# Two channel tiles of the next block's first product, taken ahead at the block ends of a decoder trunk

## The reference

```
h = h + c * rms_norm(block(rms_norm(h, g_pre)), g_post)
ffn:  f = (silu(a @ w_gate) * (a @ w_up)) @ w_down          # 1024 -> 2816 -> 1024, c = 1/2
mix:  proj = a @ w_in                                        # 1024 -> 2576
      mix = concat(pool(..), conv(..), gla(q, k, v, ..)) @ w_out   # c = 1
rms_norm(x, g) = x * rsqrt(mean(x * x, over channels) + 1e-6) * g
```

## Time and profile before

| | us |
|---|---|
| median of three runs | 1024.07 |
| profiled execution, its own time | 1023.6 |
| its span | 1021.8 |
| TensorE busy | 1012.9 (99%) |
| VectorE busy | 603.5 (59%) |
| ScalarE busy | 488.6 (48%) |
| GpSimd busy | 271.0 (27%) |

### The profile page before, as it was taken

The page is one execution under the profiler, slowest core; times in us unless marked ns, Lnnn a source line. Parts: engine busy times, 40 slices in busy tenths (PEclk is TensorE's granted clock), DMA queues, the critical chain, the costliest instruction groups (busy, mean ns, idle before and its releaser), DMA issues.

```text
span 1021.8 us, 21132 instructions
## 1 busy us (share of the span) xinstructions
PE 1012.9 (99%) x8870; PEld 983.0 (96%) x8870; DVE 603.5 (59%) x574; ACT 488.6 (48%) x537; POOL 271.0 (27%) x184
## 2 busy tenths in 40 slices
PE   9999999999999999999999999999999999999997
PEld 8999999989999999999999999999899999999886
DVE  5755453488966744554376454544889677455452
ACT  5543434456555544343455443434565665434331
POOL 0333330123402333330113333301234024333200
PEclk9999999999999999999999999999999999999999
DMA  9765545645345755336747553356453557565621
GB/s 295 244 213 164 161 134 186 211 126 164 126 149 164 225 186 170 128 113 198 219 130 233 180 164 128 123 191 216 126 165 127 158 157 247 175 195 202 194 77 42
DMA packets 164147, 173.85 MB, mean 170 GB/s; under 512 B 9316, under 2 KB 150888, under 8 KB 164088
## 3 DMA queue, kind: packets, MB, share of 16 engines
q1 hardware_dynamic: 161960, 171.01, 52.7%
q10 hardware_dynamic: 2128, 1.98, 0.7%
HBM read 171.91 MB, written 1.06 MB: 169 GB/s over the span
## 4 chain that ended last, share of the span: by engine, by line
PE 95%; ACT 1%; DMA 1%; DVE 1%; SPq 0%; issue 0%; DVEq 0%; ACTq 0%
PE ps L1295 24%; PE ps L1296 24%; PE ps L1297 24%; PE ps L1327 2%; PE ps L1328 2%; PE ps L1312 2%; PE ps L1416 2%; PE ps L1458 2%; PE ps L1496 2%; PE ps L1498 2%; PE ps L1497 2%; PE ps L1459 2%; PE ps L1643 1%; DMA raw<-in_ffn_wu 1%; PE ps L1525 1%; PE ps L1354 0%
## 5 line engine op out<-in xcount | busy, mean ns | idle before, releaser
L785 DVE TENSOR_TENSOR w_lo<-raw,w_hi 128x2048 fp32r<-128x2048 f32 (+3 forms) x175 | 385.4, 2206 | 296.9 <-ACT w_hi L514 296.4
L1295 PE MATMUL ps<-x_hi,w_hi 128*128 128x272 f32 (+2 forms) x1568 | 449.3, 287 | 0.2 <-DVE w_lo L785 0.2
L1296 PE MATMUL ps<-x_lo,w_hi 128*128 128x272 f32 (+2 forms) x1568 | 449.3, 287 | 0.0
L1297 PE MATMUL ps<-x_hi,w_lo 128*128 128x272 f32 (+2 forms) x1568 | 448.5, 286 | 0.0
L514 ACT ACTIVATE w_hi<-raw 128x2048 fp32r<-128x2048 f32 (+3 forms) x175 | 312.7, 1791 | 212.6 <-PE ps L1297 151.4
L1295 PEld LDWEIGHTS ps<-x_hi,w_hi 128*128 128x128 f32 x1568 | 295.4, 188 | 1.9 <-issue 0.9
L1296 PEld LDWEIGHTS ps<-x_lo,w_hi 128*128 128x128 f32 x1568 | 295.0, 188 | 0.1
L1297 PEld LDWEIGHTS ps<-x_hi,w_lo 128*128 128x128 f32 x1568 | 294.8, 188 | 0.0
L1213 POOL TENSOR_TENSOR up<-gate,up 128x544 f32<-128x544 f32 (+1 forms) x44 | 59.6, 1354 | 310.7 <-ACT gate L605 310.7
L1216 POOL TENSOR_TENSOR hid_lo<-up,hid_hi 128x544 f32 (+3 forms) x44 | 122.9, 2792 | 45.9 <-ACT hid_hi L609 45.9
L605 ACT ACTIVATE gate<-gate 128x544 f32<-128x544 f32 (+1 forms) x44 | 28.7, 653 | 196.7 <-DVE gate L948 196.7
(11 more groups left out here) (204 smaller groups left out, 1114.1 us busy)
## 6 DMA issues: line engine op xcount, KB each, us to landing
raw<-in_ffn_wg SPq DMA_DIRECT2D x87, 512.0 KB, 4.0
raw<-in_ffn_wu SPq DMA_DIRECT2D x87, 512.0 KB, 4.9
raw<-in_ffn_wd SPq DMA_DIRECT2D x72, 384.0 KB, 3.2
raw<-in_w_in SPq DMA_DIRECT2D x40, 512.0 KB, 4.6
raw<-in_ffn_wd SPq DMA_DIRECT2D x20, 512.0 KB, 4.7
raw<-in_w_out SPq DMA_DIRECT2D x16, 512.0 KB, 4.8
raw<-in_ffn_wd SPq DMA_DIRECT2D x28, 256.0 KB, 3.2
x_tok<-in_x SPq DMA_DIRECT2D x4, 256.0 KB, 4.9
```

Source lines behind the costliest of these rows:

```text
L785: v_.tensor_tensor(w_lo[:, slot, 0:n], raw[:, slot, 0:n], f32(w_hi[:, slot, 0:n]), ALU.subtract)\
L1295: pe.matmul(out_, wh, xh, start=first, stop=False)
L1296: pe.matmul(out_, wh, xl, start=False, stop=False)
L1297: return pe.matmul(out_, wl, xh, start=False, stop=last)
```

## The change

At each of the five block ends, tiles 2 and 3 of h are split off as `h_new = h_old + f * g_post * r_post`. TensorE multiplies the first two output tiles' weights of the next block with `h_old * g_pre` of tiles 2 and 3 (12 products, into banks 0 and 1) and with `f * g_post * g_pre` of the same tiles (12 products, into banks 6 and 7). ScalarE and VectorE make these inputs' high and low parts during the block's last stretch (`high_ahead`, `low_ahead`). VectorE later multiplies banks 6 and 7 by r_post, and joins the result with banks 0 and 1 before it uses gate or q. In the opening, tiles 2 and 3 run only for the other two output tiles, and they come last: the order of the tiles is 0, 1, 4, 5, 6, 7, 2, 3 on all engines. The five products of ones per block end are gone. The spread post root goes to banks 2 to 5; ScalarE copies it to the new tile `r_post`, and VectorE reads it there for all scales of f but the first. `both_gains` holds the products of the two gains and is made once.

```diff
             def split_h(bnd, gain, layer, t0):
-                for kk in range(KT):
-                    act.wait_ge(h_ready, 8 * bnd + kk + 1)
+                act.wait_ge(post_scaled, bnd)
+                act.activation(quarters(r_post, t0), spread_post(t0), ACT.Copy).then_inc(r_post_out, 1)
+                for n, kk in enumerate(ORDER):
+                    act.wait_ge(h_ready, 8 * bnd + n + 1)
+                    if n == 0:
+                        act.wait_ge(old_mm, bnd)
+                    if kk == AHEAD[0]:
+                        act.wait_ge(out_mm, bnd)
...
+            def high_ahead(ph, t0):
+                nx = phases[ph["b"] + 1]
+                act.wait_ge(gains_ready, 1)
+                for n, kk in enumerate(AHEAD):
+                    act.activation(x_hi[:, n, t0:T], h[:, kk, t0:T], ACT.Copy,
+                                   scale=col(PRE[nx["kind"]], nx["layer"], kk)).then_inc(old_hi, 1)
+                act.wait_ge(pair_out, 4 * ph["b"] + 2)
+                for n, kk in enumerate(AHEAD):
+                    act.activation(x_hi[:, 2 + n, t0:T], f[:, kk, t0:T], ACT.Copy,
+                                   scale=both(ph["b"], n)).then_inc(old_hi, 1)
...
+                def scale_pair(kk):
+                    v_.wait_ge(pair_out, 4 * (bnd - 1) + kk // 2 + 1)
+                    c[kk] = c[kk + 1] = mark(v_.tensor_tensor(f[:, kk:kk + 2, t0:T], f[:, kk:kk + 2, t0:T],
+                                                              tok(r_post, 2, t0), ALU.mult))
                 v_.wait_ge(post_bc, bnd)
+                v_.wait_ge(pair_out, 4 * (bnd - 1) + 1)
+                v_.tensor_tensor(quarters(f[:, 0], t0), quarters(f[:, 0], t0), spread_post(t0), ALU.mult)\
+                  .then_inc(post_scaled, 1)
+                add(0)
+                v_.wait_ge(r_post_out, bnd)
+                c[1] = mark(v_.tensor_tensor(f[:, 1, t0:T], f[:, 1, t0:T], r_post[:, t0:T], ALU.mult))
+                add(1)
+                for n in range(2, KT, 2):
+                    scale_pair(ORDER[n])
+                    add(ORDER[n])
+                    add(ORDER[n + 1])
+                v_.wait_ge(out_mm, bnd)
+                if phases[bnd]["kind"] == "mix":
+                    tq = phases[bnd]["t_out"]
+                    v_.tensor_tensor(q[:, :, tq:T], ps[:, 6:8, tq:T], tok(r_post, 2, tq), ALU.mult).then_inc(out_scaled, 1)
+                else:
+                    v_.tensor_tensor(gate[:, 0, :, t0:T], ps[:, 6:8, 0:T - t0], tok(r_post, 2, t0), ALU.mult)\
+                      .then_inc(out_scaled, 1)
+                for n in range(6):
+                    low_x(n)
...
+                        if first and bnd:
+                            v_.wait_ge(unit_used, i4 + (ua + 2))
+                            v_.wait_ge(out_scaled, bnd)
+                            n = mark(v_.tensor_tensor(gate[:, 0, :, t0:T], g_src, gate[:, 0, :, t0:T], ALU.add))
...
                 if bnd:
+                    pe.wait_ge(r_post_out, bnd)
+                    pe.wait_ge(unit_lo, u0 + 2 + RING)
+                for n, kg in enumerate(ORDER if bnd else ()):
+                    view = view_of((u0 + kg // 4) % RING)
+                    pe.wait_ge(xh_ready, 8 * bnd + n + 1)
+                    for mm in range(2 if kg in AHEAD else 0, 4):
...
+                if bnd:
+                    pe.wait_ge(out_scaled, bnd)
                     for n in range(3):
                         pe.wait_ge(sq_sum, 3 * (bnd - 1) + n + 1)
-                        last = add_tile(4, f[:, (0, 4, 6)[n]], t0, n == 0, n == 2)
+                        last = add_tile(4, f[:, ORDER[(0, 4, 6)[n]]], t0, n == 0, n == 2)
...
-                    sum_tile(bnd, t1, 1)
-                stay_warm(2, 1)
-                pe.wait_ge(post_root, bnd + 1)
-                stay_warm(3, 1)
+                nx = phases[bnd + 1]
+                pe.wait_ge(unit_lo, nx["u0"] + 1 + RING)
+                pe.wait_ge(old_lo, 4 * bnd + 2)
+                ahead_of(ph, nx, [0], 0, 0, 0)
+                sum_tile(bnd, t_end, 1)
+                ahead_of(ph, nx, [1], 0, 0, 0)
+                ahead_of(ph, nx, [0, 1], 0, 1, 0).then_inc(old_mm, 1)
                 pe.wait_ge(post_inv, bnd + 1)
                 pe.wait_ge(pair_out, 4 * bnd + 4)
-                spread_roots(t_end, post_bc)
-                stay_warm(3, WARM_BOUNDARY)
+                spread_roots(t_end, post_bc, 2)
+                pe.wait_ge(old_lo, 4 * bnd + 4)
+                ahead_of(ph, nx, [0, 1], 1, 0, 6)
+                ahead_of(ph, nx, [0, 1], 1, 1, 6).then_inc(out_mm, 1)
```

More of the change, by code:

```diff
@@ L142, in trunk @@
         r_pre = sb("r_pre", [P, T])
+        r_post = sb("r_post", [P, T])
+        both_gains = sb("both_gains", [P, len(AHEAD) * (3 * DEPTH - 1)])
         eps = sb("eps", [P, 1])
@@ L367, in spread, with lows, spread_post, both @@
             return src if n == 1 else src.unsqueeze(1).to_broadcast([P, n, 4, w])
+        def lows(ph):
+            return x_lo if ph["kind"] == "mix" else up_lo
+        def spread_post(ph_t0):
+            return ps[:, 2:6, 0:(T - ph_t0) // 4]
+        POST = {"ffn1": "ffn1_post", "mix": "mix_post", "ffn2": "ffn2_post"}
+        PRE = {"ffn1": "ffn1_pre", "mix": "mix_pre", "ffn2": "ffn2_pre"}
+        def both(bnd, n):
+            c = len(AHEAD) * bnd + n
+            return both_gains[:, c:c + 1]
         def last_of(ph, what):
@@ L801, in new_h @@
                 c = {}
[L803 to L807, removed]
                 def add(kk):
-                    v_.wait_ge(dve, c[kk])
+                    if kk == ORDER[0]:
+                        v_.wait_ge(post_scaled, bnd)
+                    else:
+                        v_.wait_ge(dve, c[kk])
@@ L827, in new_h, with low_ahead @@
                     v_.tensor_tensor(glow, ps[:, 5, 0:w4], root4[:, 0:w4], ALU.mult).then_inc(glow_out, 1)
-                for kk in range(6, KT):
-                    low_x(kk)
+                for n in range(6, KT):
+                    low_x(n)
+            def low_ahead(ph, t0):
+                nx, lo = phases[ph["b"] + 1], lows(ph)
+                for n, kk in enumerate(AHEAD):
+                    v_.wait_ge(old_hi, 4 * ph["b"] + n + 1)
+                    v_.scalar_tensor_tensor(lo[:, n, t0:T], h[:, kk, t0:T], col(PRE[nx["kind"]], nx["layer"], kk),
+                                            f32(x_hi[:, n, t0:T]), ALU.mult, ALU.subtract).then_inc(old_lo, 1)
+                for n, kk in enumerate(AHEAD):
+                    v_.wait_ge(old_hi, 4 * ph["b"] + n + 3)
+                    v_.scalar_tensor_tensor(lo[:, 2 + n, t0:T], f[:, kk, t0:T], both(ph["b"], n),
+                                            f32(x_hi[:, 2 + n, t0:T]), ALU.mult, ALU.subtract).then_inc(old_lo, 1)
             def invert(root, count, done, t0):
@@ L969, in _ @@
                                 low_unit(u, UNIT)
+                        if pair == 2:
+                            low_ahead(ph, t0)
                         if bnd == 0 and pair == 1:
                             other_parameters()
+                            for n in range(NB - 1):
+                                c1 = C[POST[phases[n]["kind"]]][0] + KT * phases[n]["layer"] + AHEAD[0]
+                                c2 = C[PRE[phases[n + 1]["kind"]]][0] + KT * phases[n + 1]["layer"] + AHEAD[0]
+                                last = v_.tensor_tensor(both_gains[:, len(AHEAD) * n:len(AHEAD) * (n + 1)],
+                                                        par[:, c1:c1 + len(AHEAD)], par[:, c2:c2 + len(AHEAD)], ALU.mult)
+                            last.then_inc(gains_ready, 1)
                             v_.wait_ge(glow_in, 16 * DEPTH)
@@ L1157, in _ @@
                     low_y(8, 7, y_head[:, 3, t1:T])
-                    for j in range(12, 17):
+                    for j in range(12, 16):
                         ahead(j)
+                    low_ahead(ph, t1)
+                    ahead(16)
                 for n in range(2):
@@ L1477, in opening, with ahead_of @@
                 if bnd:
-                    with_low(0)
-                    with_low(1)
+                    low_products()
                 else:
                     with_low(1)
+            def ahead_of(ph, nx, m_list, src, tile, bank):
+                view = up_view(nx["u0"] % RING) if nx["kind"] != "mix" else k_view(nx["u0"] % RING, 4, 512)
+                ta = nx["t_out"] if nx["kind"] == "mix" else nx["t_in"]
+                at = ta - nx["t_in"]
+                n, kk, lo = 2 * src + tile, AHEAD[tile], lows(ph)
+                for mm in m_list:
+                    last = mm3(ps[:, bank + mm, at:at + T - ta], view(w_hi, kk, mm), view(w_lo, kk, mm), x_hi[:, n, ta:T],
+                               lo[:, n, ta:T], tile == 0, src == 1 and tile == 1)
+                return last
             def last_down(d0, hid_tile, ups):
```

88 lines of the change are left out of this document (50 added, 38 removed).

## The result

| | before | after |
|---|---|---|
| median of nine runs, side by side | 1025.19 us | 1028.10 us |
| ratio, 95% interval | | 1.0033 [1.0024, 1.0042] |
| profiled execution, its own time | 1023.6 us | 1028.4 us |
| its span | 1021.8 us | 1026.6 us |

The change made the kernel slower by about 3.4 us (0.0033 x 1025.19; the two medians differ by 2.91). The forecast was 1023.7 us and no difference clear of noise; the time lies above the range's upper end of 1027.0. The kernel before gave 1025.19 here, where the forecast had started from 1024.07; from that number the same ratio would give 1027.5, still above the range.

What follows compares the result with a forecast made beforehand. TensorE, busy 99% of the span, was taken as the bound, with time to win only in fill or waits; block-end gains less late starts gave -0.4 us, 1023.2 profiled, forecast 1023.7 us median, range 1019.8 to 1027.0.

Steps and rivals of the forecast that it cites:

- the port: Block ends: VectorE's two-SBUF scales and GpSimd's adds exclude each other; eighth h tile 0.74 us later, last sum at 10.21.
- The two constants: Delays at the SBUF port: VectorE's operation ends 0.30 us after GpSimd's add, GpSimd's next add 0.63 us after that.
- Rival A: No port conflict for the scales at block ends: 3.7 us gained, 1020.4 us; chance 0.23.
- Rival B: GpSimd gets the port first, each meeting costing about 0.75 us instead of 0.35: +3.4 us, 1027.5 us; chance 0.15.
- Rival C: 12 products fewer in each opening and everything else in time: 6.3 us gained, 1017.8 us; chance 0.05.
- The rule of the Trainium skill: Two-SBUF VectorE instructions contend with GpSimd reading SBUF; first issuer holds the port throughout. Worth some 3.3 us less gain.
- the late start of the spread: Before the post root's spread: three products ahead of the last sum delay it 0.15 us after an FFN, 0.42 after a mixer.
- the forecast's -0.4: Sum over five block ends: -0.17 twice before a mixer; before an FFN, -0.2 once and +0.07 twice.
- ScalarE's 0.28 us: After an FFN, TensorE's old wait for ScalarE's square before the last sum, taken to absorb part of the three products.
- a cover of 0.04 us: Between last sum and spread: nine products, 1.13 us, fit where fill and the root wait took 1.17 us, counted as hidden.
- nothing was to be paid outside the block ends: Ahead of block ends: four ScalarE copies and four VectorE low parts priced at nothing; uncovered, copies up to 2.0 us each end.
- TensorE standing outside the block ends: Sign of error: the forecast is wrong if TensorE stands anywhere outside the block ends; no size given.

Runs made afterwards that it cites:

- d1_before_rpost: Kernel before, with ScalarE copying the spread post root to r_post in SBUF, where VectorE reads it for all scales but the first: 1025.74 us, ratio 1.0018.
- d2_before_warm: Kernel before, with one fill product moved from behind the last sum of squares to ahead of it: 1026.75 us, ratio 1.0026 to the kernel before.
- a2_move3: Kernel after, with three products moved behind the last sum of squares and three more behind the spread: 1026.43 us, ratio 1.0018 to the kernel before.
- b1_nopool: Kernel before, without GpSimd's sums of squares of h at block ends; TensorE sums all eight tiles: 1026.71 us, ratio 1.0025.
- a3_nopool: Kernel after, without GpSimd's sums of squares of h at block ends; TensorE sums all eight tiles: 1024.07 us, ratio 1.0003 to the kernel before.
- c1_move3_nopool: Kernel after, with three products moved behind the last sum and no GpSimd sums at block ends: 1022.59 us, ratio 0.9985 to the kernel before.
- c2_move3_pool2: Kernel after, three products moved behind the last sum, GpSimd making only two additions after the last h tile: 1022.15 us, ratio 0.9975 to the kernel before.
- a1_again: Kernel after, run once more without any edit: 1027.68 us, ratio 1.0034 to the kernel before.

## Why the prediction was wrong

**What held: the port and all that hangs on it.** The timeline of DVE after, the same block end as the earlier trace rows:

```profile
321.06 0.44 DVE L873 TENSOR_TENSOR f<-f,ps 128x272 f32<-128x272 f32 x1 [0.78 <-PE ps L1461]
...
324.45 0.72 DVE L869 TENSOR_TENSOR f<-f,r_post 128x544 f32<-128x544 f32 x1
325.20 1.32 DVE L864 SCALAR_TENSOR_TENSOR h<-f,par,h 128x272 f32<-128x272 f32 x2
326.44 0.72 DVE L869 TENSOR_TENSOR f<-f,r_post 128x544 f32<-128x544 f32 x1
327.19 1.30 DVE L864 SCALAR_TENSOR_TENSOR h<-f,par,h 128x272 f32<-128x272 f32 x2
328.42 0.71 DVE L889 TENSOR_TENSOR gate<-ps,r_post 128x544 f32<-128x544 f32 x1
329.05 3.76 DVE L855 SCALAR_TENSOR_TENSOR x_lo<-h,par,x_hi 128x272 fp32r<-128x272 f32 x6
```

The timeline of POOL after, beside the earlier trace rows:

```profile
324.68 1.13 POOL L1296 TENSOR_TENSOR f<-f 128x272 f32<-128x272 f32 x1 [11.81 <-DVE h L864]
326.66 1.12 POOL L1296 TENSOR_TENSOR f<-f 128x272 f32<-128x272 f32 x1 [0.86 <-DVE h L864]
328.66 2.61 POOL L1296 TENSOR_TENSOR f<-f 128x272 f32<-128x272 f32 x3 [0.88 <-DVE h L864]
```

Counted from 321.06 as the prediction counted: GpSimd's first two additions end at 4.75 and 6.72 (predicted 4.76, 6.73), the eighth tile of h at 7.43 (7.44), the last sum at 10.21 (10.21), the low products start at 10.52 (about 10.5). The two constants read off one meeting in the kernel before, 0.30 and 0.63 us, carried the whole stage. Rival A asked for additions of 0.77 us: it falls. Rival B asked for scales over 1.2 us: they take 0.72. Rival C, that the count of products holds, falls with the 0.59 us in which TensorE waits for GpSimd before the last sum (the prediction had it idle for about a microsecond). The rule of the Trainium skill, page "SBUF — State Buffer", section "Who interferes with whom", named in the prediction, agrees with d1_before_rpost: +1.9 us for one operand moved, and GpSimd's addition, begun 0.22 us behind the scale, is the one that ends late.

From the spread to the next unit the first mixer's end gained 0.32 us (14.97 to 14.65; predicted 0.35) and the first FFN's end 0.34 (17.33 to 16.99; predicted 0.32). The third gained 0.31, the last two only 0.09 and 0.16: in the kernel before, their high products already took 7.99 and 7.68 us instead of the 8.19 of the end from which I counted. In all the ends gained 1.22 us behind the spread where the prediction had 1.69.

**The step that failed: the late start of the spread.** The prediction had 0.15 us after an FFN and 0.42 after a mixer, 3 x 0.15 + 2 x 0.42 = 1.29. Measured from first sum to spread: +0.55, +0.78, +0.56, +0.48 and +0.69, together 3.06. The mechanism was named rightly (three products stand ahead of the sum for which the root waits); its size was wrong by 1.77 us, which alone turns the forecast's -0.4 us into +1.4. Among the things that were to show it right, the spread was to come 0.1 to 0.4 us later; it came 0.48 to 0.78 later. The weight loads show what was missing. PEld of the kernel before, first FFN's end, around the row:

```profile
210.58 0.28 PEld L1354 LDWEIGHTS ps<-sq_all,ones 128*32 128x32 f32 x16 [0.15 <-issue]
...
212.56 0.31 PEld L1361 LDWEIGHTS ps<-root,ones 1*128 1x128 f32 x8 [0.36 <-DVE root L834]
```

PEld of the kernel after, the same place:

```profile
211.94 0.28 PEld L1454 LDWEIGHTS ps<-sq_all,ones 128*32 128x32 f32 x16
212.31 0.19 PEld L1395 LDWEIGHTS ps<-x_hi,w_hi 128*128 128x128 f32 x1
212.42 0.19 PEld L1396 LDWEIGHTS ps<-up_lo,w_hi 128*128 128x128 f32 x1
212.54 0.19 PEld L1397 LDWEIGHTS ps<-x_hi,w_lo 128*128 128x128 f32 x1
212.88 0.16 PEld L1454 LDWEIGHTS ps<-sq_all,ones 128*32 128x32 f32 x8
...
214.13 0.19 PEld L1397 LDWEIGHTS ps<-x_hi,w_lo 128*128 128x128 f32 x1
214.47 0.31 PEld L1461 LDWEIGHTS ps<-root,ones 1*128 1x128 f32 x8
```

Within the products the loads follow each other by 0.11 to 0.13 us. From the third product's load to the sum's it is 0.34, and from the ninth's to the spread's again 0.34. A change from products of 272 columns to the small ones costs about 0.21 us, and the prediction counted products only, 0.126 each. In the kernel before, the two sums after a mixer stood side by side and paid that change once. Whether the shape of the weights or the number of columns makes it, no run separates.

- Ahead of the sum: from the first sum's load to the last one's it took 0.56 us after the FFN in the kernel before, 0.94 after the change. That is +0.38 where I had 0.15, although ScalarE's 0.28 us are gone.
- Ahead of the spread: I let the nine products hide in the wait for the root. VectorE's reciprocal, which the spread waits for, shows that they hide no longer. In the kernel before it ended at 212.46 and the spread's load came 0.10 later; in the kernel after it ends at 214.21, and the load comes at 214.47:

```profile
211.88 0.58 DVE L834 RECIPROCAL root<-mean 128x68 f32<-128x68 f32 x1
```

```profile
213.63 0.58 DVE L916 RECIPROCAL root<-mean 128x68 f32<-128x68 f32 x1 [0.35 <-ACT mean L823]
```

(first the kernel before, then the kernel after, timeline of DVE). 0.26 - 0.10 = 0.16, and 0.38 + 0.16 = 0.54 of the 0.55 measured. I had the nine products down as 1.13 us against a gap of 1.17: a cover of 0.04 us, and a term left out of 0.21.

d2_before_warm shows this with nothing of the change in it, and a2_move3 by taking it away. What a2_move3 keeps (1.14 us over five) is the term at the spread. PEld there, first mixer's end:

```profile
317.60 0.48 PEld L1454 LDWEIGHTS ps<-sq_odd,ones 128*32 128x32 f32 x16
...
319.17 0.19 PEld L1397 LDWEIGHTS ps<-x_hi,w_lo 128*128 128x128 f32 x1
319.50 0.31 PEld L1461 LDWEIGHTS ps<-root,ones 1*128 1x128 f32 x8
```

Both sums are in one row again, and the spread still stands 0.33 us behind the last product.

**The second step that failed: nothing was to be paid outside the block ends.** The prediction priced the four copies and four low parts, and all else there, at nothing; the runs show 1.5 us (3.4 by the ratio, less 1.84). It isn't the chance of one execution. The ratio less the block ends gives 1.2 to 1.9 us for the kernel after, its repeat and the four kernels made from it, and within 0.4 of zero in b1_nopool, d1_before_rpost and d2_before_warm, though each ratio is good to about 0.9 us only. The profiles agree: the span without the block ends and without the stretch ahead of the first one is 722.87 to 723.04 us in the four kernels without products ahead, and 723.97 to 724.68 in the six with them (means 722.95 and 724.44). By place:

- Each of the two middle FFNs takes 0.33 us longer: from the first product behind the first mixer's end to the first sum at the FFN's end, 332.30 to 518.83 before, 335.19 to 522.06 after, 186.53 and 186.87 us. All six profiles with products taken ahead have 186.86 or 186.87; before, b1_nopool and d2_before_warm have 186.53 or 186.54, d1_before_rpost 186.56. Together 0.66 us. It is spread over the whole FFN, and in the last FFN it isn't there. The copy to r_post and the scales that read it, alone in d1_before_rpost, don't make it. No run has the copies and low parts without the products, or the products without them, so that the cause stays open.
- The two mixers together take 168.40 to 168.62 us without products ahead and 168.87 to 169.61 with them, 0.87 us more on average. In both mixers TensorE's rows fall back by 0.10 to 0.14 us in the first 5 us; most of the rest comes behind one wait. In the first mixer VectorE waits for o_mem, which comes back by DMA: 1.40 us before, 2.11 after (timelines of DVE). Behind it TensorE waits 0.48 us for x_hi in the kernel after, and not at all there in the kernel before: TensorE standing outside the block ends was one of the prediction's own signs of being wrong.

```profile
296.06 0.79 DVE L1153 TENSOR_TENSOR v<-v,kd 128x272 f32<-128x272 f32 x2 [1.40 <-DMA kd<-o_mem]
```

```profile
298.47 0.79 DVE L1250 TENSOR_TENSOR v<-v,kd 128x272 f32<-128x272 f32 x2 [2.11 <-DMA kd<-o_mem]
```

  The mixer took 85.46 and 86.32 us. With the change the wait had 2.11, 1.92, 2.23, 1.53, 1.12 and 1.48 us in one profile each, without it 1.40, 1.51, 0.91 and 1.22. Where it was short with the change, the second mixer's wait could be long: in a3_nopool (1.53) and c1_move3_nopool (1.12) that one took 2.67 and 2.76 us, in the eight others 1.85 to 1.98, and the second mixer 83.86 and 83.94 us instead of 82.95 to 83.08. Both waits together had 3.33 to 4.20 us with the change and 2.78 to 3.49 without. Why the data come back later, no run tells, and c2_move3_pool2 (3.33) shows that they don't always.
- The start of the kernel has two forms (209.9 to 210.8 us and 211.3 to 212.2 us to the first block end), in kernels with and without the change. The profiled execution of after happened to have the long one, its repeat the short one. It explains 1.4 us of the 4.8 between the two spans. The long form stood in four of the six profiles with products ahead and in one of the four without, too few to say whether the change has a part in it.

So the sum closes: the forecast's -0.4, 1.77 at the spread, 0.47 of gain that didn't come, and the 1.49 us that the profiles show outside the block ends on average make 3.3 us, against 3.4 measured. The places are shown; the causes of the 1.5 us are not.

Smaller points. The copy to r_post ended 0.87 us after the first scale began (predicted 0.93; 215.46 + 0.40 - 214.99). The opening came 1.68 us behind the first scale, as before (322.74 - 321.06; 1.67 in the kernel before). The four copies and four low parts ahead of the block end show no price in weights that come late: among the waits of TensorE in the kernel after there is none for weights.

## What to carry to other kernels

Work put into a gap is hidden only if the instruction that ends the gap doesn't queue behind it: price each piece by what stands between it and the chain's next link, with a term for each change of kind on TensorE (0.2 us here), and don't call a cover of 0.04 us a cover. When an operand moves from PSUM to SBUF, look for the other engine's instruction that runs at the same moment; here the cure was to let GpSimd add less and later. A stage whose terms agree to 0.01 us says nothing about the stages beside it: the port stage was right and the sum had the wrong sign. And don't price at nothing what lies outside the stretch that a change edits: here it cost 1.5 us, as much as the mis-sized step.

## What the runs showed of the hardware

- TensorE's change from 272-column products to sums or a spread: 0.33 to 0.34 us between the loads instead of 0.12; with one fill product between two sums, 0.95 us from sum to sum.
- VectorE with two SBUF inputs and GpSimd exclude each other in the meetings read at these block ends: GpSimd's addition ends 0.64 and 0.62 us behind VectorE's scale in the kernel after (324.45 + 0.72 and 324.68 + 1.13; 326.44 + 0.72 and 326.66 + 1.12).
- Eight sums of single tiles on TensorE cost 0.6 us more per block end than three (4.35 to 7.26 over five), less than the meetings that they avoid in the kernel after.
- The start of the kernel comes in two forms. The timelines of PE, the kernel before and then the kernel after:

```profile
6.00 1.19 PE L1525 MATMUL ps<-ones 128*128 128x272 f32 x4
7.03 1.04 PE L1549 MATMUL ps<-cst,x_tok 128*128 128x128 f32 x8
```

```profile
6.35 2.18 PE L1645 MATMUL ps<-ones 128*128 128x272 f32 x4
8.33 1.91 PE L1669 MATMUL ps<-cst,x_tok 128*128 128x128 f32 x8
```

The same instructions at half the pace for some 4 us, though the granted clock is 1.00 between 6 and 10 us in both profiles. It doesn't come with the change alone: d1_before_rpost has the slow pace too, and a1_again and a3_nopool have the fast one. c1_move3_nopool is long as well (211.3 us) without the slow pace; there TensorE waits 0.36 us for x_hi at 9.49.
